# Value projections moved out of the attention rounds into the key selection

## The reference

```python
c_q = rmsnorm(c_q, g_cq); c_kv = rmsnorm(c_kv, g_ckv)           # 1024 x 256 each
q = (c_q @ w_uq).reshape(B, T, 8, 128)
q_lat = jnp.einsum('bthd,hdc->bthc', q, w_uk) * 128 ** -0.5
score = where(causal, einsum('bqh,bqhs->bqs', wb, relu(einsum('bqhd,bsd->bqhs', q_idx, k_idx))), -inf)
_, sel = lax.top_k(score, 256)                                   # the key selection
logits = einsum('bqhc,bqkc->bqhk', qb_lat, c_kv[sel]) + bias; p = softmax(logits)
o_lat = einsum('bqhk,bqkc->bqhc', p, c_kv[sel])
o = einsum('bthc,hcv->bthv', o_lat, w_uv)                        # w_uv: 8 heads x 256 x 128
```

## Time and profile before

| | us |
|---|---|
| median of 3 runs | 2584.31 (2578.87 to 2586.06) |
| the profiled execution's own time | 2581.38 |
| its span, first to last instruction | 2579.6 |
| key selection | about 213 to 340 |
| attention | about 341 to 602 |

### The profile page before, as it was taken

One profiled execution on the slowest core, in us unless ns is written; L12 is line 12 of the kernel. 1 busy time (PEld: TensorE's weight loads), 2 busy tenths in 40 slices (PEclk: granted clock), 3 DMA queues, 4 the chain that ended last, 5 costly groups with the idle time before them and its releaser, 6 DMA issues. The chain is left out here.

```text
span 2579.6 us, 31274 instructions
## 1 busy us (share of the span) xinstructions
PE 2401.1 (93%) x11751; PEld 2034.0 (79%) x11751; DVE 1329.7 (52%) x2124; ACT 886.2 (34%) x1375; POOL 580.2 (22%) x434
## 2 busy tenths in 40 slices
PE   7878969998999999999999989789999999999996
PEld 5757958887888888888887988668788888888885
DVE  6358956666554443334443685563743333333335
ACT  4347745545331111111111564475511111111112
POOL 2103122222422222222221211004222222222212
PEclk9786579999999999999999999899999999999997
DMA  6103400003311111111110111003211111111101
GB/s 247 57 1 122 139 25 13 28 1 132 107 41 49 50 45 45 49 49 49 49 57 25 34 33 33 17 2 115 65 47 45 47 49 49 49 49 49 49 24 66
DMA packets 44517, 141.89 MB, mean 55 GB/s; under 512 B 5744, under 2 KB 10000, under 8 KB 44048
## 3 DMA queue, kind: packets, MB, share of 16 engines
q1 hardware_dynamic: 44432, 140.77, 16.5%
HBM read 134.98 MB, written 5.77 MB: 55 GB/s over the span
## 5 line engine op out<-in xcount | busy, mean ns | idle before, releaser
L158 PE MATMUL down<-g_hi,o_hi 128*128 128x512 f32 (+1 forms) x704 | 273.3, 388 | 2.3 <-DVE work L1847 1.3
L159 PE MATMUL down<-g_lo,o_hi 128*128 128x512 f32 (+1 forms) x704 | 272.4, 387 | 0.0
L160 PE MATMUL down<-g_hi,o_lo 128*128 128x512 f32 (+1 forms) x704 | 272.4, 387 | 0.0
L1834 DVE TENSOR_TENSOR relu<-relu 128x1024 f32<-128x1024 f32 x32 | 39.6, 1238 | 331.0 <-ACT relu L1697 330.9
L158 PE MATMUL up<-m_hi,i_hi 128*128 128x512 f32 x480 | 187.3, 390 | 1.4 <-DVE m_lo L1822 1.4
L160 PE MATMUL up<-m_hi,i_lo 128*128 128x512 f32 x480 | 186.8, 389 | 0.0
L159 PE MATMUL up<-m_lo,i_hi 128*128 128x512 f32 x480 | 186.8, 389 | 0.0
L1849 DVE TENSOR_TENSOR work<-down,work 128x512 f32<-128x512 f32 x224 | 147.5, 685 | 56.8 <-PE down L160 56.8
L158 PEld LDWEIGHTS down<-g_hi,o_hi 128*128 128x128 f32 x704 | 134.0, 190 | 29.5 <-DVE work L1847 1.7
L159 PEld LDWEIGHTS down<-g_lo,o_hi 128*128 128x128 f32 x704 | 133.8, 190 | 26.6
L160 PEld LDWEIGHTS down<-g_hi,o_lo 128*128 128x128 f32 x704 | 133.8, 190 | 26.5
(11 more groups left out here) (496 smaller groups left out, 5862.9 us busy)
## 6 DMA issues: line engine op xcount, KB each, us to landing
ada<-in_ada_w SPq DMA_DIRECT2D x32, 512.0 KB, 3.6
i_raw<-in_w_ff SPq DMA_DIRECT2D x32, 512.0 KB, 3.6
o_raw<-in_w_ff SPq DMA_DIRECT2D x32, 512.0 KB, 3.6
work<-in_f_w_u SPq DMA_DIRECT2D x22, 512.0 KB, 3.6
work<-in_f_w_v SPq DMA_DIRECT2D x22, 512.0 KB, 3.6
work<-in_f_w_out SPq DMA_DIRECT2D x22, 512.0 KB, 4.3
work<-in_ada_rows SPq DMA_DIRECT2D x16, 512.0 KB, 6.2
wo_raw<-in_a_w_o SPq DMA_DIRECT2D x16, 512.0 KB, 3.6
```

Of the source, the lines that this page charges most:

```text
L158: nc.tensor.matmul(out, w_hi, x_hi, start=start, stop=False)
L159: nc.tensor.matmul(out, w_hi, x_lo, start=False, stop=False)
L160: return nc.tensor.matmul(out, w_lo, x_hi, start=False, stop=stop)
L1834: nc.vector.tensor_tensor(r[:, :], r[:, :], r[:, :], ALU.mult).then_inc(square_s, 1)
```

## The change

All eight heads' values are computed in the key selection. A new input `w_v` (1 MB) holds all value weights. SP loads it near the end of `front`, ACT casts its high parts after the scores of heads 2 and 3, and POOL subtracts the low parts. At the start of the selection PE multiplies: 16 parts (8 token tiles by two halves of 512 value columns), each of six fp32r matmuls of 512 columns, into six PSUM buffers; from the seventh part on it waits for a buffer to be copied out. ACT copies one part after each counting step from step 4 on. The modulation products stand behind all parts. In attention the third projection, its weight copy (ACT), its result copy (DVE) and the sum of `ckv` (POOL) are gone; a head's weights are 256 KB instead of 384 KB, and the four rounds are written out without a loop. The tests' outputs, which nobody reads, go into the mask's place.

```diff
 # select_keys
+        junk = mask
+        values_ps = [c.ps(st, f"values_ps{i}", [P, 512]) for i in range(VALUES_PS)]   # 6
             def _(pe):
+                for n, (j, half) in enumerate(parts):
+                    if n >= VALUES_PS:
+                        pe.wait_ge(values_out, n - VALUES_PS + 1)
+                    at, tok = slice(half * 512, half * 512 + 512), slice(j * P, (j + 1) * P)
+                    for k in range(2):
+                        mm = three_products(nc, values_ps[n % VALUES_PS][:, :], ckv_hi[:, k, tok], ckv_lo[:, k, tok],
+                                            wv_hi[:, k, at], wv_lo[:, k, at], k == 0, k == 1)
+                    mm.then_inc(values_s, 1)
                 m.products(pe)
...
+                def copy_values(n):
+                    j, half = parts[n]
+                    act.wait_ge(values_s, n + 1)
+                    nc.scalar.copy(values[:, j, half * 512:half * 512 + 512], values_ps[n % VALUES_PS][:, :])\
+                        .then_inc(values_out, 1)
                 for i in range(LAST):
                     count(i)
+                    if VALUES_AT <= i < VALUES_AT + len(parts):                       # 4, 16
+                        copy_values(i - VALUES_AT)
+                act.wait_ge(values_out, len(parts))
 # front
+            sp.wait_ge(f_s, 3)
+            sp.wait_ge(totals, 3)
+            sp.dma_start(wv_raw[:, :, :], d["w_v"]).then_inc(wv_s, 16)
...
+            for k in range(2):
+                pool.wait_ge(wv_hi_s, k + 1)
+                nc.gpsimd.tensor_tensor(wv_lo[:, k, :], wv_raw[:, k, :], f32(wv_hi[:, k, :]), ALU.subtract)\
+                    .then_inc(wv_lo_s, 1)
+            pool.wait_ge(wv_lo_s, 2)
...
+                if 2 <= h < 4:
+                    act.wait_ge(wv_s, 16)
+                    nc.scalar.copy(wv_hi[:, h - 2, :], wv_raw[:, h - 2, :]).then_inc(wv_hi_s, 1)
 # attention
-        order = [(0, "proj", n) for n in range(3)]
+        order = [(0, "proj", n) for n in range(2)]
...
-            with eng.Fori(0, ROUNDS - 1) as i:
-                body(i, False)
-            body(ROUNDS - 1, True)
+            for i in range(ROUNDS):
+                body(i, i == ROUNDS - 1)
...
-                    if n == 2:
-                        for j in range(QT):
-                            for k in range(2):
-                                mm = nc.tensor.matmul(ring[u % 2][:, j // 4, (j % 4) * P:(j % 4 + 1) * P],
-                                                      ckv[:, k, j * P:(j + 1) * P], w_v[:, k * P:(k + 1) * P],
-                                                      start=(k == 0), stop=(k == 1))
-                        mm.then_inc(full, 1)
-                        return
...
                 def logits(i, hh, qt):
                     u = place[hh, "logits", qt]
-                    pe.wait_ge(free, i * PER + (u + 1))
+                    pe.wait_ge(free, i * PER + max(u + 1, 4))
...
-                        mm = nc.tensor.matmul(out[qt // 4][:, ...], proj_v[hh][:, s],
+                        mm = nc.tensor.matmul(out[qt // 4][:, ...], values[:, j, v],
```

More of the change, by code:

```diff
@@ L170, with select_keys @@
 ROWS = QT - FIRST_SCORED
-def select_keys(c, d, score, mask):
+def select_keys(c, d, score, turn, mask, values, ckv_hi, ckv_lo, wv_hi, wv_lo):
     nc = c.nc
@@ L194, in select_keys @@
     LAST = FIRST_BIT + 23
+    VALUES_PS, VALUES_AT = 6, 4
+    parts = [(j, half) for j in range(QT) for half in range(2)]
     def at(t, qt):
@@ L489, in front @@
         c.sb(wide, "w2_raw_rest", [P, KT * 2 * P - BUCKETS // 4 - 3 * P])
+        with ExitStack() as early:
+            wv_raw = c.sb(early, "wv_raw", [P, 2, HEADS * P])
         sq = [c.sb(wide, f"square{i}", [P, T]) for i in range(2)]
@@ L500, in front @@
     mask = c.sb(first, "key_mask", [P, MASK_W])
-    score = c.sb(idx, "score", [P, MASK_W])
     with ExitStack() as early:
         q = c.sb(early, "q_idx", [P, IDX_HEADS, T], F32R)
+    values = c.sb(first, "values", [P, QT, HEADS * P])
+    score, turn = (c.sb(idx, n, [P, MASK_W]) for n in ("score", "tie_test"))
+    c.sb(idx, "up_to_kv_weights", [P, T // 2])
+    wv_hi, wv_lo = (c.sb(idx, n, [P, 2, HEADS * P], F32R) for n in ("wv_hi", "wv_lo"))
     A, B, C, S = pair
@@ L532, in front @@
                            "score_masked"))
+    wv_s, wv_hi_s, wv_lo_s = (c.sem(n) for n in ("wv_loaded", "wv_hi_done", "wv_lo_done"))
     with st, nc.Block() as block:
@@ L973, in _, with attention @@
             dve.wait_ge(ckv_lo_s, 2)
-    return cq_hi, cq_lo, ckv_hi, ckv_lo, mask, window, score
-def attention(c, d, cq_hi, cq_lo, ckv_hi, ckv_lo, mask, window, o, wo_raw):
+    return cq_hi, cq_lo, ckv_hi, ckv_lo, mask, window, score, turn, values, wv_hi, wv_lo
+def attention(c, d, cq_hi, cq_lo, ckv_hi, ckv_lo, mask, window, values, o, wo_raw):
     nc = c.nc
@@ L1018, in attention @@
                 if hh == 0 and qt == EARLY:
-                    order += [(1, "proj", n) for n in range(3)]
+                    order += [(1, "proj", n) for n in range(2)]
                 order.append((hh, "logits", qt))
@@ L1095, in project @@
                 def project(i, hh):
-                    for n in range(3):
+                    for n in range(2):
                         project_one(i, hh, n)
@@ L1177, in project @@
                             .then_inc(proj_hi_s, 1)
-                    act.wait_ge(full, i * PER + (place[hh, "proj", 2] + 1))
                     if hh == 0:
                         weights(i, 1)
-                    elif not isinstance(i, int):
+                    elif i < ROUNDS - 1:
                         weights(i + 1, 0)
@@ L3298, in build_program @@
             with ExitStack() as idx:
-                cq_hi, cq_lo, ckv_hi, ckv_lo, mask, window, score = front(c, d, work, first, idx)
-                select_keys(c, d, score, mask)
+                cq_hi, cq_lo, ckv_hi, ckv_lo, mask, window, score, turn, values, wv_hi, wv_lo = front(c, d, work, first,
+                                                                                                     idx)
+                select_keys(c, d, score, turn, mask, values, ckv_hi, ckv_lo, wv_hi, wv_lo)
             c.end_stage()
@@ L3303, in build_program @@
                 wo_raw = [c.sb_right(early, f"wo_raw{i}", [P, KT * P]) for i in range(2)]
-            attention(c, d, cq_hi, cq_lo, ckv_hi, ckv_lo, mask, window, work, wo_raw)
+            attention(c, d, cq_hi, cq_lo, ckv_hi, ckv_lo, mask, window, values, work, wo_raw)
         xs = c.sb(ctx, "x", [P, KT, T2])
@@ L3345, in lay_out @@
     uq, uk, uv = a["a_w_uq"][0], a["a_w_uk"][0], a["a_w_uv"][0]
-    heads = np.empty((HEADS, P, 3, 2, P), np.float32)
+    heads = np.empty((HEADS, P, 2, 2, P), np.float32)
+    w_v = np.empty((P, 2, HEADS, P), np.float32)
     for h in range(HEADS):
@@ L3351, in lay_out @@
             heads[h, :, 1, k] = uk[h].T[rows]
-            heads[h, :, 2, k] = uv[h][rows]
+            w_v[:, k, h] = uv[h][rows]
     gates = np.zeros((P, 2, LRU_T, P), np.float32)
@@ L3382, in lay_out @@
         "a_w_qi": tiles(w_qi.reshape(-1, IDX_HEADS * P)).transpose(1, 0, 2).reshape(P, -1),
-        "w_heads": heads.reshape(HEADS, P, 6 * P), "a_w_o": tiles(a["a_w_o"][0]),
+        "w_heads": heads.reshape(HEADS, P, 4 * P), "w_v": w_v.reshape(P, 2, HEADS * P),
+        "a_w_o": tiles(a["a_w_o"][0]),
         "rel_bias": a["rel_bias"], "one_hot": one_hot,
```

23 lines of the change are left out of this document (6 added, 17 removed).

## The result

The changed kernel takes 2606.08 us (median of 4 runs, 2599.17 to 2607.13), the kernel before 2582.32 us beside it (4 runs, 2578.87 to 2586.06): a ratio of 1.0086, with a 95% interval of 1.0071 to 1.0100. It is slower, by about 22 us by the ratio. The profiled execution took 2607.13 us, its span 2605.3 us.

What follows compares the result with a forecast made beforehand. PE was taken to bound the attention, DVE's and ACT's tests the selection. From 2581.4 us: + 1.0 (front) + 34.5 (modulation) - 17.3 + 1.3 (attention) = 2600.9, predicted as 2601 us, range 2589 to 2608.

Steps and rivals of the forecast that it cites:

- The slack and the shift: Key selection: PE has 10.7 us to spare before DVE wants the modulation's sum, but the modulation shifts by 45.2 us.
- When the modulation starts: Key selection: the modulation starts only after value part 16, at 262.3 instead of 217.1.
- The 0.7 us for nine copies: Key selection: ACT's value copies lengthen the nine test steps before the tenth copy by 0.7 us in all.
- How long it takes: Modulation on PE: 512 records at 0.2135 us each, at half clock throughout, 109.3 us.
- Rival 1: Modulation: PE stays at full clock, it ends before DVE's sum, and the time is 2568 us; chance 0.12.
- The late term, +34.5: Key selection: the late modulation makes the stage end at 374.2 instead of 339.7, 34.5 us later.
- Front: Before the selection: ACT's casts are hidden, POOL's differences may slow DVE's score sums; 1 us taken.
- The attention, row by row: Attention savings: entry 1.0, first head 2.5, three later rounds 1.0 each, second head 2.7 four times; 17.3 us together.
- the sign that was set in advance: Profile after: from first projection to last output copy, the attention is 14 to 20 us shorter.
- The clock in the attention: Attention: new PE waits make falls to half clock likelier, 0 to 9 us; one fall taken, 1.3 us.
- Rival 2: Attention: the new waits cost the clock each time, seven falls, 7 to 8 us more, 2608 us; chance 0.10.
- Writing out the rounds: Attention: four rounds written out without a loop cost nothing, as the fourth was written out already.

Runs made afterwards that it cites:

- e1: Changed kernel with six value parts, then the modulation, then the other ten parts on PE in the selection; 2578.05 us, 0.9976 of before.
- e5: Changed kernel with every second product of the modulation left out; 2574.78 us, 0.9964 of before.
- e3: Changed kernel with nine unread 128x512 products on PE in the wait ahead of each round's first logits; 2594.82 us, 1.0043 of before.
- a0: The changed kernel run once more, unaltered, beside later kernels; 2597.84 us, 1.0069 of before.
- e4: Changed kernel with tile 14's transposes and tile 13's value products put ahead of the next round's first logits; 2592.55 us, 1.0035 of before.
- e6: Changed kernel without the value products on PE in the selection, ACT copying scores instead; 2571.66 us, 0.9958 of before.
- b1: The kernel before with only the four attention rounds written out without the loop; 2583.59 us, 1.0017 of before.
- c1: Changed kernel with the new orders of e1 and e4 together; 2570.58 us, 0.9961 of before.
- c2: c1 with three late value copies between the last penalties and e3's unread products in the first round only; 2572.34 us, 0.9969 of before.

## Why the prediction was right, and where it was off

The forecast of slower by 17 us (2601.0, range 2589 to 2608) held: 2606.08 us, and 2597.84 us in the repetition. That it came so close is in part luck: the wait for the modulation was too large in it and the clock's price too small. Point by point:

- **The slack and the shift.** Right. The slack of 10.7 us met the late modulation, DVE's sum waited 28.2 us for it, and the tail behind the sum is unchanged. e1 and e5 show the cause.
- **When the modulation starts.** Predicted 262.3 (and 1.0 for the front), measured 262.6 with a selection that began 2.0 us later. The 0.7 us for nine copies measured nothing: a step with a copy is 3.19 us, and the pause hides it. The values ran at full clock: the last part took 1.5 us and not 2.6, which takes another 1.1 us off.
- **How long it takes.** Predicted 109.3 us, measured 104.9. Rival 1 was right in its first few microseconds: the one-column products did begin at 1.00. They read 0.73 from 265 to 270 and 0.50 after, so the full clock at the start saved 4.4 us and not 55. The late term, +34.5, should have been 28.2; this is the first term that was mis-sized.
- **Front.** Predicted +1.0, measured +2.0. It is not shown to be of the change: kernels with the same front began the selection between 210.0 (e3) and 216.2 (a0), before at 213.5.
- **The attention, row by row.** Right to 0.3 us at each point: second head 2.9 for 2.7, between rounds 1.0 for 1.0, first round 2.3 for 2.5, entry 1.3 for 1.0. These make 4 x 2.9 + 3 x 1.0 + 2.3 + 1.3 = 18.2 us, where 17.3 were predicted, and 16.9 of them lie in the attention. But only 7.3 us arrived there, and the sign that was set in advance, an attention 14 to 20 us shorter, failed.
- **The clock in the attention.** This term of the sum failed in size: "none to seven" falls at 1 to 1.5 us, "of which I take one, 1.3 us". No row gave that price. The trace has six falls in place of one: the first costs 5.1 us of clock and the five others 1.7 us each, and the clock lost grew by 15.6 - 3.5 = 12.1 us. In time this is less. By difference it is 16.9 - 7.3 = 9.6 us. The kernels with the same attention give an estimate: 15.6 us lost make 247.8 us and 9.1 lost make 243.0, so one lost microsecond costs about 0.74 us, and 12.1 of them 9 us: the upper end of the 0 to 9 us that the sum allowed. Rival 2, with 7 to 8 us more, had this right, and got a chance of 0.10. What was held against it, that the rounds before had the same gaps, was wrong, since PE had had 3.7 us of value products where the waits are now. Filling them brings back 3 to 9 us (e3 and e4, against e1, e5 and e6 or against the changed kernel).
- **Writing out the rounds.** Predicted nothing; in the attention that holds. The 4.1 us in the rest of the program are measured in b1 too, and open.

So errors of opposite sign meet. By the table the end of the selection came 5.2 us earlier than predicted and the entry took 0.3 us less, while the attention took 7.7 us more and the rest 4.1 us more: 6 us in all for the profiled execution.

## What to carry over

Before work is moved to an engine that "has time", find out what the stage's end waits for on that engine, and put the new work behind it, not ahead: here the order of the same products decides between 22 us lost and 6 us won. When work is taken off PE, look at what it covered: the four waits of 2.4 us that opened here stood for 9.5 us without work, and the clock behind them for 9 us more by the estimate above. Other work that is ready can go into them; here it made the attention 2.8 us (c1 against e1) to 9.1 us (e4 against the change) shorter.

## What the runs showed of the hardware

- A stream of one-column fp32 products without a pause does not keep TensorE's clock. At 1.00 when it began (in the changed kernel 262.3 to 265), it read 0.73 in the next 5 us and 0.50, which is 1.2 GHz, for the 97 us after. e1 gave the same: 0.88, then 0.50. The Trainium skill (TensorE: Matmul & The Clock Gate, Why this matters for your kernels) asks for an engine that is kept busy; these traces disagree for such products, whose busy share was 1.00.

```profile
224.00:229.00 5.00, 5.00 (x42) 5.00 (x42) 4.89 (x13) 4.45 (x11) 1.61 (x8) 0.88 0.46 120
229.00:234.00 5.00, 5.00 (x25) 5.00 (x25) 4.79 (x13) 4.85 (x11) 1.01 (x6) 0.50 0.66 205
```

- Wide products, on the other hand, kept 1.00 with PE busy 10.32 of 20 us (240 to 260 in the changed kernel).
- An idle wait of 2.37 us on PE was followed by half clock in the first round of all nine kernels that left it empty (3.4 to 5.1 us of clock lost), and by none in e3, where nine unread products filled it. In c2, with the same filler, 1.7 us were lost.
- The same instructions can keep or lose the clock. Six kernels with one and the same attention lost 9.1 to 15.6 us of clock and took 243.0 to 247.8 us. The length less the clock lost is not a constant either: it is 232 to 236 us in the eleven kernels without the value projections, and highest where least clock was lost.
